# Full 64x64 tiles in place of 32x32 ones in the inversion levels of a recurrent mixer

## The reference, cut to what matters

```
def step(state, inp):
    r_t, w_t, k_t, v_t, ka_t, kb_t = inp
    sa = einsum('bhvk,bhk->bhv', state, ka_t)
    state = state * w_t + sa * kb_t + v_t * k_t      # outer products
    return state, einsum('bhvk,bhk->bhv', state, r_t)
```

## Time and profile before

| what | us |
|---|---|
| median of 3 runs | 2860.01 (2858.05 to 2860.39) |
| span of the profiled execution, first to last instruction | 2853.6 |
| by difference, around the span | 6.4 |
| first products, L815 | 1044.7 to 1074.7 of the span |
| levels, L826 | 1074.7 to 1170.5 |
| chunk loop, L815 | 1170.5 to 1211.7 |

### The profile page before, as it was taken

How to read it: one execution, slowest core, us unless ns; L and a number is a source line. 1 busy time by engine, 2 the same in 40 slices (tenths; PEclk the granted TensorE clock), 3 DMA queues, 4 the chain that set the end, 5 groups by cost and what they waited for, 6 DMA issues and landing times.

```text
span 2853.6 us, 37543 instructions
## 1 busy us (share of the span) xinstructions
PE 2322.3 (81%) x16012; PEld 1581.9 (55%) x16016; DVE 776.6 (27%) x1449; ACT 345.6 (12%) x600; POOL 8.7 (0%) x13
## 2 busy tenths in 40 slices
PE   6999879999997995799999995787666666665665
PEld 5887668888886885688886775651111111111111
DVE  4545434563003362421024218550000000000001
ACT  1102231011001311111012210120000000000001
POOL 0000000000001000000000000000000000000000
PEclk9999989999998995799999997877767768768777
DMA  8887225894443320035342220369999999999996
GB/s 344 347 359 327 105 117 235 350 363 187 159 142 138 143 95 5 4 122 185 136 162 75 88 72 17 125 248 417 418 418 417 416 418 418 418 417 416 417 418 282
DMA packets 114096, 709.24 MB, mean 249 GB/s; under 512 B 10832, under 2 KB 10960, under 8 KB 44496
## 3 DMA queue, kind: packets, MB, share of 16 engines
q1 hardware_dynamic: 114000, 707.80, 62.1%
HBM read 706.71 MB, written 1.05 MB: 248 GB/s over the span
## 4 chain that ended last, share of the span: by engine, by line
PE 62%; DMA 25%; DVE 7%; SPq 3%; issue 2%; ACT 1%; DVEq 0%; ACTq 0%
DMA ring<-in_w 15%; PE ps L656 11%; PE ps L663 11%; PE ps L670 11%; DMA sq<-in_w 8%; PE ps L699 5%; PE ps L1020 4%; SPq L558 3%; PE ps L815 2%; PE ps L1200 2%; PE ps L826 2%; PE ps L1238 1%; PE ps L1227 1%; PE ps L629 1%; PE ps L1018 1%
## 5 line engine op out<-in xcount | busy, mean ns | idle before, releaser
L656 PE MATMUL ps<-hT,arena 128*128 128x256 f32 x1408 | 326.5, 386 | 10.7 <-ACT hT L1314 10.7
L663 PE MATMUL ps<-hT,arena 128*128 128x256 f32 x1408 | 318.3, 379 | 0.0
L670 PE MATMUL ps<-hid,arena 128*128 128x256 f32 x1408 | 311.1, 379 | 0.0
L656 PEld LDWEIGHTS ps<-hT,arena 128*128 128x128 f32 x1408 | 272.8, 194 | 54.4 <-issue 16.2
L670 PEld LDWEIGHTS ps<-hid,arena 128*128 128x128 f32 x1408 | 267.5, 190 | 36.4
L663 PEld LDWEIGHTS ps<-hT,arena 128*128 128x128 f32 x1408 | 267.5, 190 | 36.4
L1200 PE MATMUL ps<-ring,arena 128*32 128x512 f32 x1024 | 169.0, 760 | 76.7 <-DMA ring<-in_w 75.1
L1286 ACT ACTIVATE arena<-ps 128x512 f32<-128x512 f32 (+5 forms) x152 | 96.0, 641 | 1059.8 <-PE ps L1217 319.6
L1200 PE MATMUL ps<-arena 128*32 128x512 f32 x768 | 143.6, 838 | 87.8 <-DMA arena<-in_w 87.8
L1675 DVE TENSOR_TENSOR hid<-sil,ps 128x256 f32<-128x256 f32 x88 | 37.0, 421 | 578.9 <-ACT sil L1324 578.7
L1648 DVE CUSTOM_DVE_ANT_0 sq<-arena 128x1024 f32<-128x1024 f32 x168 | 194.5, 1220 | 0.0
(11 more groups left out here) (349 smaller groups left out, 2126.7 us busy)
## 6 DMA issues: line engine op xcount, KB each, us to landing
arena<-in_w SPq DMA_DIRECT2D x192, 1024.0 KB, 24.0
ring<-in_w SPq DMA_DIRECT2D x128, 1024.0 KB, 20.7
arena<-in_ada SPq DMA_DIRECT2D x96, 1024.0 KB, 10.4
ring<-in_ring_w SPq DMA_DIRECT2D x52, 1024.0 KB, 4.9
arena<-in_ffn_gate SPq DMA_DIRECT2D x44, 1024.0 KB, 5.7
arena<-in_ffn_up SPq DMA_DIRECT2D x44, 1024.0 KB, 6.3
arena<-in_ffn_down SPq DMA_DIRECT2D x44, 1024.0 KB, 4.8
hT<-in_w SPq DMA_DIRECT2D x32, 1024.0 KB, 18.1
```

What stands on the lines that cost most here:

```text
L656: last = mm(ps[:, ft, 0:T], gate3[:, kt, ft * P:(ft + 1) * P], h3[:, kt, :], start=kt == 0, stop=kt == KT - 1)
L663: last = mm(ps[:, ft, T:2 * T], up3[:, kt, ft * P:(ft + 1) * P], h3[:, kt, :], start=kt == 0, stop=kt == KT - 1)
L670: last = mm(acc(m), down3[:, ft, m * P:(m + 1) * P], hid3[:, ft, :], start=False, stop=True, skip_group_check=True)
```

## The change

In all five levels `heads` takes the place of `blocks`. A call then makes 16 matmuls of 64x64, one for each head, over the full matrices; the masks, the copies, the banks, the waits and their order stay. `blocks` is removed.

```
-            def blocks(bank, lhs, rhs, to=None):
-
-                for kt in range(KT):
-                    for q in range(4) if to is None else (0, 2):
-
-                        r, i, j, o = (q, q % 2, q % 2, q) if to is None else (q, 1, 0, q + 1) if to == "below" else (q + 1, 0, 1, q)
-                        r, o = slice(32 * r, 32 * r + 32), slice(32 * o, 32 * o + 32)
-                        last = mm(ps[o, bank, kt * HD + 32 * j:kt * HD + 32 * j + 32], lhs[r, kt, 32 * i:32 * i + 32],
-                                  rhs[r, kt, 32 * j:32 * j + 32], start=True, stop=True, skip_group_check=True)
-                return last
...
                         pe.wait_ge(sem("rw_T"), n + c + 1)
                         if lev == 1:
                             pe.wait_ge(sem("rw_first_a"), 9 + c)
-                        blocks(c, c_ab[c], c_t[c], "below" if lev == 5 else None).then_inc(sem("rw_Y"), 1)
+                        heads(c, c_ab[c], c_t[c]).then_inc(sem("rw_Y"), 1)
                     for c in range(NCH):
                         pe.wait_ge(sem("rw_Ys"), n + c + 1)
                         if lev == 1:
                             pe.wait_ge(sem("rw_first_d"), 17 + c)
                         if lev < 5:
-                            blocks(c, c_tt[c], c_y[c])
-                        blocks(4 + c, c_y[c], c_tt[c], "above" if lev == 5 else None).then_inc(sem("rw_Z"), 1)
+                            heads(c, c_tt[c], c_y[c])
+                        heads(4 + c, c_y[c], c_tt[c]).then_inc(sem("rw_Z"), 1)
```

## The result

| | before | after |
|---|---|---|
| median of 4 runs, us | 2860.2 (2858.05 to 2863.84) | 2808.9 (2806.84 to 2811.34) |
| ratio, 95% interval | | 0.9823 (0.9809 to 0.9837) |
| span of the profiled execution, us | 2853.6 | 2806.9 |

The profiled execution of after took 2808.7, so what lies around its span is 1.8 us, not 6.4. The difference between the two spans is 46.7 us.

What follows compares the result with a forecast made beforehand. The prediction took the levels to be bound by the arrival of instructions. Levels -41.1 and chunk loop -1.3 summed to -42.4, so 2860.0 became 2817.6 us; eight in ten within 2811 to 2826.

Steps and rivals of the forecast that it cites:

- The mechanism: Levels: bound by instruction arrival, one block of 256 each 3.71 us; 14 blocks in place of 26; stage -41.1 us.
- Matmuls: Levels after the change: 1792 records at 29.3 ns each, at full clock, 52.5 us.
- Supply: Levels after the change: TensorE waits where an instruction block takes over 3.75 us; 1.2 us, bounds 0 to 3.5.
- Copies, the end: Levels: copies all covered, nothing added; at the end 0.8 us wait for the last masked copy plus 0.2 passage.
- Chunk loop: Loop after the levels: starts at full instead of half clock, -1.3 us, bounds -1.3 and 0.
- Behind: Rest of the span behind the mixer: shifts with TensorE; clock changes may fall differently, +-3 us, nothing in the sum.
- Clock before the change: Levels before: idle time was said to have taken the clock down, 0.54 on average against 1.00 before the stage.
- the median lies 6.4 us above the span: Whole kernel: span 2853.6 becomes 2811.2; starting from 2860.0, the forecast time became 2817.6 us.
- Blocks without overlap (1): Levels: each block requested only when the last is consumed, some 1.8 us gap after each; -17, 2843 us; chance 0.05.
- Gaps that stay (2): Levels: 43.1 us idle stays whole, for a cause other than supply; +0.8, 2861 us, no change; chance 0.03.
- The clock that doesn't hold (3): Levels and chunk loop: clock falls to 1.2 GHz and stays, 55 ns a record; +28, 2888 us; chance 0.03.
- Something given back later (4): Behind the mixer: a stretch loses 8 us or more to clock or an unseen wait; 2826 to 2835 us; chance 0.05.

Runs made afterwards that it cites:

- run 4: Kernel before, but levels 1 to 4 make their 32x32 products for every second pair of heads only; levels 51.5 us.
- run 5: Kernel before, with each 32x32 matmul of levels 1 to 4 issued as two of 16 columns, all computed; levels 181.5 us, total 2941.5 us.
- run 7: 64x64 version with only 32 of 64 weight columns and 32 of 64 moving columns per matmul in the levels; levels 52.2 us.
- after_timed: The 64x64 version unchanged, timed in five rounds and profiled again; 2809.9 us against 2857.6, ratio 0.9826; traced span 2810.8 us.
- after_b: The 64x64 version unchanged, profiled once more; levels 53.4 us, span 2810.9 us.
- after_c: The 64x64 version unchanged, a further profiled execution; levels 53.7 us, span 2813.4 us.
- slim32: Same as run 7: 64x64 version with 32 of 64 weight columns and 32 of 64 moving columns in the levels; levels 52.2 us.
- half32: Kernel before, but levels 1 to 4 make only two of the four diagonal 32x32 blocks per pair of heads; levels 53.3 us, total 2811.4 us.
- lev5_32: 64x64 tiles in levels 1 to 4, the 32x32 tiles of before in level 5, all computed; median 2814.0 us, ratio 0.9837, levels 54.2 us.
- narrow64: 64x64 version, but each matmul in the levels computes only the first 32 of its 64 columns, weights kept at 64x64; levels 53.2 us.
- halfpairs: Same as run 4: kernel before, levels 1 to 4 computed for every second pair of heads only; levels 51.5 us.
- run 3: Same as half32: kernel before, two of four diagonal 32x32 blocks in levels 1 to 4; levels 53.3 us, total 2811.4 us.

## Why the prediction was wrong

**The mechanism was right.** The levels were bound by the arrival of instructions: runs 4, 5 and 7 hold the array's pace, the tile's shape and the number of instructions apart, and while the array passes a block in less than 3.45 us only the last sets the length (14 blocks 51.5 to 54.3 us, 26 blocks 95 to 101, 50 blocks 181.5). In after the two bounds are level, and the array's stream is the one that shows. The rule of the Trainium skill that crossing a block's boundary is mostly hidden ("Runtime: NRT & Kernel Launch", Instruction fetch mechanics) does not hold where 256 small instructions pass in less than 3.45 us.

**Matmuls:** 1792 records at 29.3 ns, 52.5 us; after's unbroken row has 1920 records in 56.71 us, 29.5 ns. Right, for a reason that I hadn't given (the weight columns).

**Supply:** 1.2 us of waits forecast; the four executions of after lie between 0.1 below and 0.8 over the gapless sum of 53.5 us. Oversized by 0.4 to 1.3.

**Copies, the end:** right, 0.82 us of wait, none for a copy within the levels. So the levels came to 53.8 us for 54.7 forecast, -42.0 for -41.1.

**Chunk loop:** -1.3 forecast, -1.9 measured. The direction and the cause were right: the loop starts at full clock in all four executions of after. The other 0.6 us are the last call, at half clock before: it ran at full clock in after and after_timed (loops of 39.8 us), at half clock in after_b and after_c (40.4). It differs between executions of the same program, and the forecast's -1.3 had no term for it.

**Behind:** 0 +- 3 forecast, -0.5 on average and -4.0 in the first trace. The range for it was too small for one execution.

**Clock before the change:** "the idle time has also taken the clock down" is not borne out by the runs as it stands. It fell behind gaps in before, but slim32 has a similar share of idle time (20.6 of 52.2 us, against 43.9 of 95.8) and kept 1.00, and half32 was busy for 47.26 of 53.3 us and had 0.56. Nothing in the sum rests on it, since 29.3 ns at full clock came true.

**The step that failed** is the last one, "the median lies 6.4 us above the span": I took 6.4 as a fixed cost around the span and put it on top of the kernel after. In after the median lies 2.0 us above the traced span (2808.9 - 2806.9), and in all 38 executions for which both numbers are on record the time is 1.7 to 3.0 us above its own span. The 8.7 us between 2817.6 and 2808.9 are then: 4.4 around the span, 4.0 behind the mixer (forecast 0 +- 3), 0.9 in the levels, 0.6 in the chunk loop, less 1.2 ahead of the levels, where the program is the same and which I had at nothing.

The rest of the 6.4, some 4 us, said that the traced execution was quicker than the three timed ones. Half of it is this: its span of 2853.6 lies 2.3 below the mean of the five traces, 0.9 of that in the levels (95.8 against 96.7) and 1.3 ahead of them. The other half is that the first executions of before were slow ones, with a median of 2860.2 against 2857.9 over all 20. So a part of the measured 51.3 is the draw of executions: by the traces the change is worth 45.4, 3.0 more than forecast, and by medians 47.7 to 48.0.

I also let the supply's period spread from 3.45 to 4.00 in the bounds of after, where 14 blocks hide it under the stream, and never in before, where 26 blocks carry it in full. The levels' term should have been -42.8 with a bound down to -46 (99.8 - 53.8). With that bound in place of -42.3 the range's lower end would be about 2807, an estimate, and 2808.9 inside; but that would have been luck, for the levels of this pair gave -42.0, and the miss came from elsewhere.

**The rivals.** Blocks without overlap (1): out, no gaps behind 3.75 us blocks. Gaps that stay (2): out; two calls of before do have 128 records, which the argument against this rival passed over, but in run 4 a call has 32 and the bursts still 128. The clock that doesn't hold (3): out, 1.00 throughout. Something given back later (4): not seen. The array rule (35.6 us of array time before, 52.5 after) is right about the array, and irrelevant while the supply is the bound; nearly halving the instructions was worth more than the better packing.

**No better version** came out: at 64x64 the stream (3.75 us a block) and the supply (3.6 to 3.8 on average) are level, so a quicker array gains nothing (lev5_32, narrow64 and slim32 all have levels of 52 to 54 us) and fewer instructions at the same pace of the array would gain nothing either, if its stream kept its length. That last one wasn't tried, nor was a version with fewer instructions of more weight columns.

## What to carry to other kernels

Where straight code has many tiny matmuls, divide the time by blocks of 256 instructions: if TensorE runs in bursts of 128 matmul records with "issue" gaps and the period is 3.5 to 4 us, the count of instructions is the cost. A wider, more wasteful tile that halves the count then halves the time, as long as the array passes its records within the same period (29 ns each, as the 64x64 tiles just do). Before sizing a gain from one trace, subtract the span from the median: it was 1.7 to 3.0 us here within one execution, and more means that the traced execution and the timed ones differ. Then a second trace is worth more than a finer sum.

## What the runs showed of the hardware

- With 64 weight columns a 64x64 f32 record took 29.3 ns whether 64 or 32 columns moved; with 32 weight columns on 64 rows 17 ns.
- With two 32x32 tiles in turn a record took 17 ns at full clock (half32, 2.18 us / 127).
- Four 32x32 tiles in turn passed a record in 15 ns at half clock, with 32 moving columns or with 16, two tiles in 28 (runs 4, 5 and 3).
- The granted clock doesn't go by idle time alone: in slim32 TensorE was idle for 20.6 of 52.2 us and kept 1.00; in halfpairs it was idle for 21.6 of 51.5 and had 0.56. In half32 it was idle for only 6.0 of 53.3 us and had 0.56. Why was not looked into.
